# Sums over channels with 64 equal moving columns instead of one, between the sub-layers of a two-layer trunk

## What is computed

```python
def rmsnorm(x, g):
    xf = x.astype(jnp.float32)
    y = xf * lax.rsqrt(jnp.mean(xf * xf, axis=-1, keepdims=True) + EPS)
    return (y * g.astype(jnp.float32)).astype(x.dtype)

def pre_norm(x, mod, j, g):
    return rmsnorm(x, g) * (1 + mod_chunk(mod, 3 * j + 1)) + mod_chunk(mod, 3 * j)

def post_residual(x, out, mod, j, g, w):
    return x + w * mod_chunk(mod, 3 * j + 2) * rmsnorm(out, g)

# for each layer and sub-layer, for the prompt (p) and for the sample (s):
xp = post_residual(xp, swiglu(pre_norm(xp, mod_p, 0, norm_pre[l, 0]), ffn_w_in[l, 0], ffn_w_out[l, 0]),
                   mod_p, 0, norm_post[l, 0], 0.5)
...
```

## Time and profile before

| | |
|---|---|
| median of 3 runs | 1703.81 us (1703.18 to 1704.05) |
| the profiled execution, its own time | 1695.97 us |
| its span | 1694.0 us |
| mean granted clock of TensorE | 0.979 |
| PE busy | 1630.7 us, 96% |
| DVE busy | 835.4 us, 49% |
| ACT busy | 695.5 us, 41% |

### The profile page before, as it was taken

The page is one execution under the profiler, slowest core; times in us unless marked ns, Lnnn a source line. Parts: engine busy times, 40 slices in busy tenths (PEclk is TensorE's granted clock), DMA queues, the critical chain, the costliest instruction groups (busy, mean ns, idle before and its releaser), DMA issues.

```text
span 1694.0 us, 27671 instructions
## 1 busy us (share of the span) xinstructions
PE 1630.7 (96%) x11325; PEld 1586.9 (94%) x11325; DVE 835.4 (49%) x1323; ACT 695.5 (41%) x1205; POOL 45.7 (3%) x46
## 2 busy tenths in 40 slices
PE   5999999999899999999999999999999999999997
PEld 4999999998778988999999899999989999999997
DVE  5543433563445977434334644343463776343333
ACT  3433333454443456433334633333363356333332
POOL 2000000010110000000000000000000000000000
PEclk9999999999989999999999999999999999999998
DMA  9633366776986125433334443436454365343310
GB/s 329 223 128 132 130 199 213 231 207 160 267 213 210 50 85 177 138 130 129 112 112 149 161 138 124 129 108 211 148 186 133 110 220 176 129 132 125 116 44 37
DMA packets 255919, 260.51 MB, mean 154 GB/s; under 512 B 6625, under 2 KB 253826, under 8 KB 255826
## 3 DMA queue, kind: packets, MB, share of 16 engines
q1 hardware_dynamic: 249664, 251.67, 46.0%
q0 software_dynamic: 1184, 3.11, 2.0%
q10 hardware_dynamic: 4978, 4.41, 0.8%
HBM read 256.56 MB, written 2.62 MB: 153 GB/s over the span
## 4 chain that ended last, share of the span: by engine, by line
PE 83%; DVE 8%; DMA 3%; issue 2%; ACT 2%; POOL 1%; ACTq 0%; SPq 0%; DVEq 0%; POOLq 0%
PE bank L402 24%; PE bank L404 23%; PE bank L403 23%; DMA RAW<-in_mod_w 3%; PE bank L1444 2%; DVE X L1045 1%; DVE HL L1011 1%; PE bank L1488 1%; DVE OUTF L1041 1%; PE bank L1495 1%; DVE WL L369 1%; PE bank L432 1%; PE bank L1708 1%; PE bank L434 1%; PE bank L433 1%
## 5 line engine op out<-in xcount | busy, mean ns | idle before, releaser
L369 DVE TENSOR_TENSOR WL<-RAW,WH 128x1024 fp32r<-128x1024 f32 (+1 forms) x335 | 401.4, 1200 | 699.0 <-ACT WH L355 698.8
L355 ACT ACTIVATE WH<-RAW 128x1024 fp32r<-128x1024 f32 (+1 forms) x344 | 358.1, 1045 | 658.6 <-PE bank L404 641.6
L402 PE MATMUL bank<-HH,WH 128*128 128x384 f32 x1664 | 561.7, 338 | 2.2 <-ACT MIX L664 2.2
L404 PE MATMUL bank<-HH,WL 128*128 128x384 f32 x1664 | 559.4, 336 | 0.0
L403 PE MATMUL bank<-HL,WH 128*128 128x384 f32 x1664 | 559.4, 336 | 0.0
L402 PEld LDWEIGHTS bank<-HH,WH 128*128 128x128 f32 x1664 | 313.2, 188 | 4.7 <-ACT MIX L664 2.6
L403 PEld LDWEIGHTS bank<-HL,WH 128*128 128x128 f32 x1664 | 313.1, 188 | 0.0
L404 PEld LDWEIGHTS bank<-HH,WL 128*128 128x128 f32 x1664 | 313.0, 188 | 0.0
L402 PE MATMUL bank<-AH,WH 128*128 128x384 f32 x704 | 237.3, 337 | 0.0
L403 PE MATMUL bank<-AL,WH 128*128 128x384 f32 x704 | 236.6, 336 | 0.0
L404 PE MATMUL bank<-AH,WL 128*128 128x384 f32 x704 | 236.6, 336 | 0.0
(11 more groups left out here) (225 smaller groups left out, 1462.6 us busy)
## 6 DMA issues: line engine op xcount, KB each, us to landing
RAW<-in_ffn_w_in SPq DMA_DIRECT2D x88, 1024.0 KB, 5.1
RAW<-in_mod_w SPq DMA_DIRECT2D x72, 1024.0 KB, 7.3
RAW<-in_ffn_w_out SPq DMA_DIRECT2D x32, 1024.0 KB, 5.2
RAW<-in_ab_w_in SPq DMA_DIRECT2D x16, 1024.0 KB, 10.2
RAW<-in_ffn_w_out SPq DMA_DIRECT2D x16, 768.0 KB, 4.7
RAW<-in_cv_w_in SPq DMA_DIRECT2D x12, 1024.0 KB, 5.9
RAW<-in_ab_w_out SPq DMA_DIRECT2D x4, 1024.0 KB, 13.7
RAW<-in_cv_w_out SPq DMA_DIRECT2D x4, 1024.0 KB, 5.2
```

The costliest lines, as they stand in the source:

```text
L355: e.activation(WH[:, (2 * m + b) % 4, 0:nk, :], RAW[:, p, 0:nk, b * P:(b + 1) * P], ACT.Copy).then_inc(half_hi, 1)
L369: e.tensor_tensor(WL[:, k, 0:nk, :], RAW[:, p, 0:nk, b * P:(b + 1) * P], WH[:, k, 0:nk, :].bitcast(F32), ALU.subtract).then_inc(half_ready, 1)
L402: e.matmul(out, WH[:, k, kk, :], xh(kk), start=(first and kk == 0), stop=False)
L404: mm = e.matmul(out, WL[:, k, kk, :], xh(kk), start=False, stop=(last and kk == nk - 1))
```

## The change

The moving operand of every sum has 64 equal columns instead of one. ONES[:, 0:64] takes the place of ONES[:, 0:1]; W7's two weights, and CC's gain, are repeated 64 times by an access with step zero. In bank 0 the sums of out squared and of y squared then lie in turn, in 128 columns for each piece of tokens (so the first group writes every second column, and the closing group 128 columns at once); in bank 1 there are 64 columns for each piece. The three readers take one column of each piece, now 128 columns apart. The number, the order and the waits of instructions on every engine are as before.

```diff
-                root(bank[0][:, 0:6].rearrange("p (t k) -> p k t", k=2)[:, 0, :], 0, (stat_done, 2 * s + 1))
+                root(bank[0][:, 0:NT].rearrange("p (t n) -> p n t", t=TOKS)[:, 0, :], 0, (stat_done, 2 * s + 1))
...
-                sum_y2, sum_xy = bank[0][:, 0:6].rearrange("p (t k) -> p k t", k=2)[:, 1, :], bank[1][:, 0:3]
+                sum_y2, sum_xy = (bank[j][:, 0:NT].rearrange("p (t n) -> p n t", t=TOKS)[:, 1 - j, :] for j in range(2))
...
-            def sums(B, src, weights, columns, opens=False, closes=False):
+            def sums(out, src, weights, opens=False, closes=False):
 
                 for t in range(TOKS):
-                    mm = pe.matmul(B[:, columns(t)], src[:, t * P:(t + 1) * P], weights(t),
+                    mm = pe.matmul(out(t), src[:, t * P:(t + 1) * P], weights(t),
                                    start=opens and t == 0, stop=closes and t == TOKS - 1)
...
-                one = lambda t: ONES[:, 0:1]
+                one = lambda t: ONES[:, 0:64]
                 group = lambda t: min(t, 1)
+                wide = lambda t: slice(t * P, (t + 1) * P)
+                y2 = lambda i: (lambda t: bank[0][:, wide(t)].rearrange("p (n k) -> p k n", k=2)[:, i, :])
+                xy = lambda t: bank[1][:, t * P:t * P + 64]
                 pe.wait_ge(sq_added, 6 * s + 6)
-                sums(bank[0], ACC, one, lambda t: slice(2 * t, 2 * t + 1), opens=True)
+                sums(y2(0), ACC, one, opens=True)
                 if s < 5:
                     pe.wait_ge(y_added, 6 * s + 6)
-                    sums(bank[0], RSTD, one, lambda t: slice(2 * t + 1, 2 * t + 2))
+                    sums(y2(1), RSTD, one)
                     pe.wait_ge(xy_added, 6 * s + 6)
-                    sums(bank[1], ROOT, one, lambda t: slice(t, t + 1), opens=True)
+                    sums(xy, ROOT, one, opens=True)
                 pe.wait_ge(out_sq, 8 * s + 8)
                 if s < 5:
-                    sums(bank[0], SQ[:, 1, :], lambda t: W7[:, group(t), :], lambda t: slice(2 * t, 2 * t + 2),
+                    sums(lambda t: bank[0][:, wide(t)].rearrange("p (n k) -> p n k", k=2), SQ[:, 1, :],
+                         lambda t: W7[:, group(t):group(t) + 1, :].broadcast_to([P, 64, 2]),
                          closes=True).then_inc(stat_done, 1)
                     pe.wait_ge(xy_done, 8 * s + 8)
-                    sums(bank[1], TT[:, 1, :], lambda t: CC[:, s, 7, group(t):group(t) + 1],
-                         lambda t: slice(t, t + 1), closes=True).then_inc(stat_done, 1)
+                    sums(xy, TT[:, 1, :], lambda t: CC[:, s, 7, group(t):group(t) + 1].broadcast_to([P, 64]),
+                         closes=True).then_inc(stat_done, 1)
                 else:
-                    sums(bank[0], SQ[:, 1, :], one, lambda t: slice(2 * t, 2 * t + 1),
-                         closes=True).then_inc(stat_done, 1)
+                    sums(y2(0), SQ[:, 1, :], one, closes=True).then_inc(stat_done, 1)
```

## The result

| | before | after |
|---|---|---|
| median of 6 timed runs each | 1703.33 us (1698.68 to 1704.05) | 1692.35 us (1685.55 to 1694.34) |
| ratio | | 0.9937, 95% interval 0.992 to 0.9955 |
| profiled execution, its own time | 1695.97 us | 1692.43 us |
| its span | 1694.0 us | 1690.6 us |
| mean granted clock | 0.979 | 0.985 |

The prediction said 1697.8 us and a range down to 1693.2; the measured median lies 0.85 us under the range. The two profiled executions differ by only 3.4 us of span. Both numbers need an explanation, and they do not have the same one.

The account below looks back on a forecast made before the run. TensorE's 384-column matmuls were taken as most of 1694.0 us, with VectorE's loop setting the turnovers' pace. Held clock -6.11 and sum latency +0.1 gave -6.0: 1703.81 to 1697.8 us, range 1693.2 to 1702.5.

Parts of the forecast that it names:

- The clock in the turnovers: First SQ sum to end of second spread: 64 columns hold the clock at 1.00, saving 6.11 us over six turnovers.
- The step of the sums: Issue of sums in turnovers: the weight load sets the 0.112 us step, 64 columns add 0, at most 3 us.
- The rival in which load and stream do not overlap: Turnover sums pay for streaming on top of weight loads: 10.7 us more, net +4.6, 1708.4 us; chance 0.05.
- The readers: Root and lines 1067 and 1069 read three elements at another spacing: 0, bounded by 0.4 us either way.
- A second fall: Before L432, behind the turnovers: three falls in five again, term nothing; ends 4.8 us less, 3.2 us more.
- the second fall comes less often: Before L432, one or none in five turnovers has the clock fall: 1694.6 to 1693.0 us; chance 0.08.
- The give-back: Clock falls before L432 in all five, or more in the attention stage: net -2.8 us, 1701.0 us; chance 0.15.
- Carrying the profile to the median: Whole kernel: the difference within the profiled 1695.97 us, 0.46% below the median 1703.81, applied to that median unchanged.
- within: Whole-kernel outcome not told from no change, about 0.2% or 3.4 us; chance 0.25.

Follow-up runs that it names:

- second profile of before: Unchanged kernel of before, no edit, profiled again (1701.44 us) and timed again: median 1700.44 us, ratio 1.0003.
- the two later comparisons: Changed kernel with 64 columns, no further edit, timed twice more against before: 1695.19 us (0.9968) and 1697.34 us (0.9979).
- the filler before L432: Six unread 128-column fp32 matmuls added in PE's wait before L432: on before 1698.36 us (0.9956), on the changed kernel 1691.94 us (0.9924).

## Why the prediction was right in its mechanism and wrong in its number

**The clock in the turnovers: right, in place and size.** 19 of 25 turnovers fall in five profiles with one column, none of 35 in seven profiles with 64. The term of 6.11 us, read from five pairs of rows, less 0.1, came out as 6.0 between the two first profiles: 5.3 in five turnovers and 0.7 at the end. It was not a lucky pair: from the first sum to the first L432 the five turnovers together take 130.6 to 133.7 us in the five profiles with one column (mean 132.1), and 126.3 to 126.4 in the seven with 64, so 5.7 us less in the mean, where the forecast had 5.76 for these five. The last turnover gave more than the 0.35 forecast, since the low clock that followed there was shorter too (6.8 us instead of 10.2), and turnover 1 less, 2.5 instead of 2.95. There the full-clock path was mis-read: 4.15 us of turnover 3 was taken for it too, but from the first SQ sum to the end of the second spread turnover 1 takes 4.53 us at full clock with one column (657.76 to 661.36 + 0.93 in the second profile of before) and 4.52 with 64. The two errors nearly cancel, and that is luck.

**The step of the sums: right.** 18 one-column sums took 2.06 us in turnover 3 before; after, 18 of 64 columns take 2.12 (turnover 0's row, the same in turnovers 2 and 3):

```profile
326.32 2.12 PE L1488 MATMUL bank<-ONES,SUMS 128*128 128x64 f32 x18
```

The six with SQ, 128 columns wide, take 0.89 us instead of 0.81, and the root begins 0.10 us later behind the first sum. The second spread ends 6.08 us behind the first sum in turnover 3 before and 6.07 after, so nothing of that is left there. The rival in which load and stream do not overlap, at +4.6 us, is out. So is the rule behind it as the prediction read it: in the Trainium skill, "TensorE: Matmul & The Clock Gate", Part 3, "The mechanism", a weight load would not overlap with a matmul on the same rows of the array (the same section makes an exception of a background weight buffer, which the prediction left out), and here the stream of 64 columns added 0.06 us to 18 of them.

**The readers: right.** Line 603 from the bank has 262 ns after, 263 before.

**A second fall: the step that failed.** The prediction took three falls before L432 again, the same as before, and put the term at nothing. The profile after has one, which is 3.1 us of the 5.5 us by which the forecast missed. The rest: before's median had come down by 0.5 us with three more runs, other pieces of the two profiles give 0.3, and 1.6 us are not placed. (That sum leaves out the +6.0 us of the attention stage, which most profiles of before have as well.) The recorded rival that comes nearest is "the second fall comes less often", 1694.6 us with one fall, and it had the chance 0.08.

The number of these falls is not a property of the kernel that one profile can show: three profiles of the changed kernel have one, four and five, and two with 32 and 16 columns and no filler five and four. Between none and five lie 5 x 1.59 = 8 us, more than the main term. Whether the five turnovers of one execution fall together or each by itself these few profiles do not show. The first comparison was at the low end: its profile has one fall, its six runs 47 us at 0.50, against 53 and 57 in the two later ones, and its gain is 11.0 us against 4.9 and 3.9. The mean of the three ratios is 0.9961, -6.6 us. That it lies next to the forecast's -6.0 is luck, since the second falls, as the next paragraph shows, take some of it back on average. The first interval and the third do not even meet (0.9955 and 0.9961), so one comparison's interval is too narrow a measure of this kernel.

The give-back that I named as a rival does exist: 7 of 20 turnovers with one column have the second fall, 10 of 15 with 64. By those shares, an estimate, it costs (0.67 - 0.35) x 5 x 1.59 = 2.5 us of what the first remedy brings, which leaves 3.5 us: near the 4.9 and 3.9 us of the two later comparisons, while with those falls out of both kernels the wide sums brought 6.4. Fifteen turnovers in three executions are few, so the share is not settled; that a filler takes all of them away (25 turnovers, none) is.

**Carrying the profile to the median: the second step that failed.** I said that the profile was 0.46% below the median and carried the difference unchanged. A wait for weights that its execution lacked, and four of the five profiles with one column have, is the largest part of it: the attention stage takes 289.8 us without the wait and 295.8 to 298.1 with it. But the two next profiled executions of before, which have the wait, took 1701.44 and 1699.54 us, so 2 to 4 us up to the median of 1703.33 are not explained by it; that median may be of another chip than theirs, which is not on record. The wait did not touch the term of the change. The falls before L432 in that profile were not usual either: three of five, where the next profiles of before have one and two.

**Two slips in the prediction's own sums.** The forecast and the rarer fall have 0.58 and 0.08, and "a little" was to go from each over the border; that is under 0.66, not 0.70, and "within" is then over 0.29, not 0.25. And the range is said to take in both ends of the second falls, but it starts at 1693.2 where that rival ends at 1693.0.

**What stays open.** Why the executions of the first comparison had less time at 0.50 than those of the later ones: its runs of before have no clock on record, so nothing shows how many falls before L432 they had. Why the filler before L432 gave the kernel of before twice what the profiles' shares say. And why the weights for the fifth step are late in most executions and not in all.

## What to carry to other kernels

A short piece of one-column matmuls between long dense ones can be the place where TensorE loses its clock, and the loss is paid behind it, in whatever is next on the path. Here widening the moving operand under the same weight loads kept the clock and cost nothing on the path. After one such fall is mended, look at the next wait of PE, since falls there may become more frequent (7 of 20 here, then 10 of 15). And when falls make up a few tenths of a per cent, take several profiles before pricing anything from one, and cut each into the same stages: the same program showed one, four and five of them, and a wait of 5 us elsewhere came and went.

## What the runs showed of the hardware that was not expected

With six filler matmuls of 128 columns in a wait of 1.87 us, the clock was at 1.00 through the 24 matmuls behind it in 25 turnovers of 25; without them, with 1 or 64 columns in the sums, it fell there in 17 of 35. They cost no time, since PE stood still there. A microsecond less at 0.50 went with about 0.4 to 0.5 us less time over the timed runs of before (slopes of span against time at 0.50: 0.39 over 35 runs on chip A, 0.47 over 24 on chip B, 0.46 over 17 on chip C; the smaller sets of the other kernels scatter from 0.25 to 0.59), a little under the half that work throughout would give. The profile calls PE busy nearly throughout both in a stretch of one-column sums that is followed by 0.50 (3.40 of 3.40 us in the earlier trace rows) and in one with sums of 64 columns that is not (6.12 of 6.14 us in turnover 2 after). The Trainium skill, "TensorE: Matmul & The Clock Gate", section "What's actually happening", lets the gate go by how busy the engine has been; these runs do not agree if that is the busy time that the profile shows, since it is the same in the two stretches and the clock is not.
